# Loading the second layer's V, Z and O weights as pairs of 256 columns: a two-layer decoder step on one core

## The reference

```python
for l in range(DEPTH):                       # DEPTH = 2
    h = rmsnorm(x, g_pre[l]) * (1 + scale) + shift      # shift, scale, gate = silu(c) @ w_ada + b_ada
    y = branch(h)                            # l = 0: attention, l = 1: mLSTM
    x = x + gate * rmsnorm(y, g_post[l])

def mlstm_branch(h, w_in, b_if, g_head, w_out, S0, n0, m0):
    proj = h @ w_in                          # (2048, 8208): q 1024, k 1024, v 2048, o 2048, z 2048, gates 16
    ...                                      # 8 heads: dk = 128, dv = 256; memory S <- a S + k v^T, read by q
    hn = rmsnorm_per_head(hs) * g_head * sigmoid(o)
    out = hn * silu(z)
    return out @ w_out, S, n, m
```

## Time and profile before

| | |
|---|---|
| median of 3 runs | 2271.52 us (2266.96 to 2273.0) |
| profiled execution | 2274.41 us |
| its span, first to last instruction | 2272.8 us |
| TensorE matmuls busy | 2170.9 us (96% of the span) |
| VectorE busy | 940.9 us (41%) |
| ScalarE busy | 677.5 us (30%) |
| DMA from the SP queue | 247.87 MB, 39.6% of 16 engines' span |
| mean granted TensorE clock | 0.979 of full speed |

### The profile page before, as it was taken

How to read it: one execution, slowest core, us unless ns; L and a number is a source line. 1 busy time by engine, 2 the same in 40 slices (tenths; PEclk the granted TensorE clock), 3 DMA queues, 4 the chain that set the end, 5 groups by cost and what they waited for, 6 DMA issues and landing times.

```text
span 2272.8 us, 37219 instructions
## 1 busy us (share of the span) xinstructions
PE 2170.9 (96%) x15828; PEld 1857.0 (82%) x15828; DVE 940.9 (41%) x1430; ACT 677.5 (30%) x1135; POOL 74.9 (3%) x125
## 2 busy tenths in 40 slices
PE   5899999999999999998899999999799999999998
PEld 2689999988999555567889999999799999985576
DVE  4434645456474422234443434443243434353223
ACT  4213534435252311126221222222222222231121
POOL 1000000000000100000000000000000000001000
PEclk8999999999999999998999999999899999999999
DMA  8972222232221788854425243534343344428622
GB/s 316 384 249 80 59 75 75 65 87 57 78 57 56 261 269 286 287 173 142 73 69 117 68 118 74 112 66 94 73 104 81 100 86 94 96 83 301 220 76 98
DMA packets 290435, 298.86 MB, mean 131 GB/s; under 512 B 8705, under 2 KB 213753, under 8 KB 288649
## 3 DMA queue, kind: packets, MB, share of 16 engines
q1 hardware_dynamic: 279504, 247.87, 39.6%
q0 software_dynamic: 10496, 48.45, 6.0%
q10 hardware_dynamic: 290, 0.32, 0.1%
HBM read 277.58 MB, written 23.11 MB: 132 GB/s over the span
## 4 chain that ended last, share of the span: by engine, by line
PE 84%; DMA 9%; DVE 3%; ACT 2%; issue 1%; ACTq 0%; DVEq 0%; SPq 0%
PE PJ L852 48%; PE PJ L1135 16%; DMA raw<-in_w_in_mlstm 6%; PE MX L1063 3%; DMA obuf<-in_w_ada 2%; PE PJ L876 2%; PE MX L992 1%; PE MX L1001 1%; PE MX L1101 1%; PE MX L1015 1%; ACT w_hi L1386 1%; PE MX L1269 1%; DVE w_lo L1842 1%; PE MX L955 1%; PE MX L1326 1%
## 5 line engine op out<-in xcount | busy, mean ns | idle before, releaser
L852 PE MATMUL PJ<-h_hi,w_hi 128*128 128x272 f32 x3200 | 684.8, 295 | 8.6 <-issue 6.9
L852 PE MATMUL PJ<-h_hi,w_lo 128*128 128x272 f32 x3200 | 667.5, 290 | 0.3 <-issue 0.3
L852 PE MATMUL PJ<-h_lo,w_hi 128*128 128x272 f32 x3200 | 665.6, 290 | 0.0
L852 PEld LDWEIGHTS PJ<-h_hi,w_hi 128*128 128x128 f32 x3200 | 507.0, 190 | 25.6 <-issue 20.8
L852 PEld LDWEIGHTS PJ<-h_lo,w_hi 128*128 128x128 f32 x3200 | 508.6, 191 | 7.0 <-issue 7.0
L852 PEld LDWEIGHTS PJ<-h_hi,w_lo 128*128 128x128 f32 x3200 | 505.6, 191 | 0.6 <-issue 0.6
L1842 DVE TENSOR_TENSOR w_lo<-raw,w_hi 128x2048 fp32r<-128x2048 f32 x106 | 242.9, 2292 | 389.0 <-ACT w_hi L1386 388.8
L1386 ACT ACTIVATE w_hi<-raw 128x2048 fp32r<-128x2048 f32 x106 | 202.3, 1909 | 86.9 <-DMA raw<-in_w_in_mlstm 64.2
L1135 PE MATMUL PJ<-w_hi,h_hi 128*128 128x512 f32 x512 | 216.1, 422 | 3.5 <-DVE w_lo L2117 2.3
L1135 PE MATMUL PJ<-w_hi,h_lo 128*128 128x512 f32 x512 | 202.9, 396 | 0.0
L1135 PE MATMUL PJ<-w_lo,h_hi 128*128 128x512 f32 x512 | 202.2, 395 | 0.0
(11 more groups left out here) (380 smaller groups left out, 2038.5 us busy)
## 6 DMA issues: line engine op xcount, KB each, us to landing
arena<-in_w_ada SPq DMA_DIRECT2D x64, 1024.0 KB, 5.2
raw<-in_w_in_mlstm SPq DMA_DIRECT2D x64, 1024.0 KB, 15.7
raw<-in_w_in_attn SPq DMA_DIRECT2D x40, 1024.0 KB, 5.8
obuf<-in_w_ada SPq DMA_DIRECT2D x32, 1024.0 KB, 11.4
raw<-in_w_out_attn SPq DMA_DIRECT2D x16, 1024.0 KB, 7.5
raw<-in_w_out_mlstm SPq DMA_DIRECT2D x16, 1024.0 KB, 5.2
arena<-in_state_C POOLq DMA_DIRECT2D x8, 1024.0 KB, 15.9
out<-arena POOLq DMA_DIRECT2D x8, 1024.0 KB, 5.9
```

The source lines that it names most:

```text
L852: last = mm(PJ[:, 2 * pair + f, 0:HT], w, h[:, k, HT * f:HT * f + HT], start=(k == 0 and n == 0), stop=(k == KT - 1 and n == 2))
```

## The change

The order of a head's units becomes Q K V V Z Z O O. The two raw buffers become the two halves of one tile, `raw_all`. Q and K are loaded as before. For V, Z and O, `load_pair` brings both units' 256 columns at once: half 0 holds k tiles 0 to 7, half 1 holds k tiles 8 to 15, each a DMA of 1 MB in pieces of 256 columns, 1 KB. `w_source` picks the 128 columns of one unit out of all sixteen k tiles, for `round_hi` and `split_lo`. The waits follow from the shared tile: a pair waits until the unit just before it has been split; ACT waits for both halves; the next head's Q, and the first block of the output projection, wait until the last O has been split; and the second O's Tanh waits until VectorE has used the first one's.

```diff
-L1K = "QKVVZOZO"
+L1K = "QKVVZZOO"
...
-        raw = [sb(f"raw{i}", [P, D]) for i in range(2)]
+        raw_all = sb("raw", [P, 2 * D])
+        raw = [raw_all[:, D * i:D * i + D] for i in range(2)]
...
+        def w_source(ph, e):
+
+            if ph == "l1" and 2 <= e < len(L1K):
+                return raw_all.rearrange("p (k n) -> p k n", k=KT)[:, :, P * (e % 2):P * (e % 2) + P]
+            return raw[slot_of(ph, e)].rearrange("p (k n) -> p k n", k=KT)
...
-                split = fixed(sp, unit_no(ph, it, e, j - 1))
+                split = fixed(sp, unit_no(ph, it, e, j - 1 + (ph == "l1" and e == 0 and it[0] is not None)))
...
-                    sp.wait_ge(lo_done, UNIT0[ph] + u - 1)
+                    sp.wait_ge(lo_done, UNIT0[ph] + u - (0 if l and u == 0 else 1))
...
+            def load_pair(it, e, col):
+
+                split = fixed(sp, unit_no("l1", it, e))
+                sp.wait_ge(xt_done, 5)
+                sp.wait_ge(lo_done, split)
+                for half in range(2):
+                    sp.dma_start(raw[half].rearrange("p (k n) -> p k n", k=KT // 2),
+                                 win1[:, KT // 2 * half:KT // 2 * (half + 1), ds(col, DV)]).then_inc(w_in[half], 16)
+
...
-                    load("l1", it, e, 0, win1[:, :, ds(h * width + (start[kind] + P * seen[kind]), P)])
+                    if kind in "QK":
+                        load("l1", it, e, 0, win1[:, :, ds(h * width + start[kind], P)])
+                    elif seen[kind] == 0:
+                        load_pair(it, e, h * width + start[kind])
...
+                if ph == "l1" and 2 <= e < len(L1K):
+                    other = e + 1 - 2 * (e % 2)
+                    act.wait_ge(w_in[slot_of(ph, other)], landed_at(ph, it, other))
...
-                fn(w_hi[s][:, :], raw[s][:, :], ACT.Copy).then_inc(hi_done, 1)
+                fn(w_hi[s][:, :].rearrange("p (k n) -> p k n", k=KT), w_source(ph, e), ACT.Copy).then_inc(hi_done, 1)
...
                 if kind == "O":
+                    if seen:
+                        act.wait_ge(*freed_at("l1", it, e - 1))
...
-                    tt(w_lo[s][:, :], raw[s][:, :], w_hi[s][:, :].bitcast(F32), ALU.subtract)\
-                        .then_inc(lo_done, 1)
+                    tt(w_lo[s][:, :].rearrange("p (k n) -> p k n", k=KT), w_source(ph, e),
+                       w_hi[s][:, :].bitcast(F32).rearrange("p (k n) -> p k n", k=KT), ALU.subtract).then_inc(lo_done, 1)
```

## The result

The changed kernel takes 2380.18 us in the median of 4 runs (2375.65 to 2385.31); the kernel before, on the same chip, 2272.26 us in 4 (2266.96 to 2274.9). The ratio is 1.0479, with a 95% interval of 1.045 to 1.0507. The direction and the range were forecast; the change was forecast as +33 us and measured as +108 us. The profiled execution took 2385.31 us, its span 2383.7.

A forecast was written before the change was run, and what follows sets the result against it. Six heads were taken as bound by matmuls, two (0 and 4) by loads. Waits of 48 us, 72 with the clock, less the present 39.2 gave +33 us: 2304 us, range 2232 to 2400 us.

The forecast's parts named there:

- The ceiling, 39.2 us: Heads 0 and 4, over head 2's 115.49 us: the most that better loading can give back, 39.2 us.
- the rival in which the pairs escape: Wide pieces escape the slow pitch: pairs land within 14.6 us in every head, no waits, 2232 us; chance 0.15.
- The price of a pair: V, Z, O loads: a pair takes what its head's first V load takes now (head 0: head 4's value); chance 0.40.
- The two factors behind it (1.28 and 0.8): Pair loads: 1 KB pieces cost 1.28 times as much, closely following loads 0.8; the product is about 1.
- V and Z, 14.7 + 21.2 = 35.9 us of waits: Pair times above the room of 15.9 us in V and 14.6 us in Z, summed over the heads.
- State traffic, 12 us "in all": V window, where GpSimd stores and reloads 1 MB of state: 12 us more waiting in all, between 0 and 60.
- O: none: O pairs: no waits, as each has 22.1 us of room before O's first unit starts on TensorE.
- The clock, half as much again: TensorE after waits: the lower clock adds half as much again, making 48 us of waiting 72 us.
- "Z Z O O moves no work": Unit order Z Z O O instead of Z O Z O: moves no work, costed at nothing.
- The next head's Q, costed at nothing: Q held back until the last O is split: 24.2 us of room against a 15.7 us median load, no cost.
- the output block: Final output projection's first block, held back by one unit of over 12 us, in fast 2 KB pieces: no cost.
- Bytes alone: Rival: a pair costs two loads in a row at 0.8 each, 2449 to 2557 us; bytes or above 1.28: chance 0.20.

The follow-up runs named there:

- the kernel with short rows: Changed kernel with all second-layer unit loads taken from the first layer's input weights, rows 20,480 instead of 32,832 bytes apart: 2231.78 us.
- Without state traffic: Changed kernel with GpSimd's per-head store and reload of the samples' memory state cut from 1 MB to 4 KB each: 2337.65 us.
- the memory steps first: Changed kernel with ScalarE and VectorE doing the previous unit's memory step ahead of the next unit's rounding and splitting, from the fifth unit on: 2315.42 us.

## Why the prediction was off, step by step

- **The ceiling, 39.2 us: right.** The heads of the kernel with short rows take 930.3 us, 37.0 less than the 967.3 of before, and its 2231.78 us is the 2232 of the rival in which the pairs escape.
- **The price of a pair: right in the mean.** Without state traffic, 15.5 us against 15.7; 21.9 in head 4 against 21.5, and up to 3.9 us off in the others. The two factors behind it (1.28 and 0.8) came from far rows, so that they cancel as they did is partly luck.
- **V and Z, 14.7 + 21.2 = 35.9 us of waits: right in sum.** Without state traffic the waits ahead of units are 40.0 us: 13.8 for V and 26.3 for Z.
- **State traffic, 12 us "in all": mis-sized.** It lengthens the V pairs of heads 1 to 7 by 3.8 to 8.2 us, and costs 24.1 us of waits ahead of units (64.1 less 40.0) and, since the heads shift, about 11 more at the memory steps: 43 us of time. The text had 60 as a bound. Its 12 is what 7.5 us a head leaves over the slack of heads 3, 5 and 7 (3.7 + 3.3 + 5.0); the other heads got nothing, on the strength of heads 2 and 6, whose second V load was fast. Head 3's 7.5 us for all of heads 1 to 7 would have made 42; ahead of V alone it was 34.9 (48.7 less 13.8). With this and O's waits the odd heads, which were to stay near 115.5 us, took 122 to 144.
- **"O: none": the step that failed.** I measured O's window up to the unit's first matmul, 22.1 us (22.2 by the earlier trace rows). What needs the landing first is the memory step behind the rounding, on ScalarE's and VectorE's programs, and its window was 12.4 us in six heads and 16.4 and 16.7 in heads 0 and 4. The text named the queue ("behind ScalarE's wait for both halves stand the memory steps") and dismissed it because TensorE needs them "only in Z and O"; but the O pair is awaited just there. Measured: 28.3 us of waits where the sum had none. With 12.4 us for the window, the forecast's own prices would have given 33 (an estimate: what the first V loads of the earlier trace rows take above 12.4 us, head 0 at head 4's value).
- **The clock, half as much again: right for the whole.** The heads lie 145.9 us above the 930.3 with 97.1 us idle, a factor of 1.50; before, 37.0 us with 25.9, 1.43. By cause it differs: 65 us for 32 of waits at the memory steps, 43 for 35 with the state's traffic.
- **"Z Z O O moves no work" at no cost: wrong in the other direction.** It gives 23 us, by the columns that are in flight together.
- **The next head's Q, costed at nothing: the same slip, small.** Its 24.2 us of room ran to Q's first matmul. No unit Q waits for its load, but memory step 6 stands behind Q's rounding and waited 3.7 us, once, in head 3. With the 28.3 us of O these are the 32.0 us that putting the memory steps first removed, for 65 us of time.
- **Costed at nothing, and right:** the output block (from the heads' end to the end of the span 247.2 us, before 248.7), the strided reads (1910 and 2291 ns, before 1909 and 2292).
- **The rivals.** Bytes alone: no, half the pieces at equal bytes take about 0.7 of the time. The Trainium skill, "DMA: Bandwidth & Descriptors", section Why small descriptors are slow, gives by an estimate 35 cycles against 2 x 19 for that, 0.92; the measurement decides. Wide pieces escape: they do from the short rows and not from these. The Trainium skill, same page, section Latency and other measured facts, reports copies slowed at row pitches of 2 MiB and more, and full speed again at 4 KiB over 4 MiB. The prediction set this against the rival, but the k tiles here lie 8 KiB over 4 MiB, so the rule spoke neither way, and no run here shows its case.

With the waits of 40 + 24 + 32 + 1 = 97 us in place of 48, the forecast's own arithmetic gives 97 x 1.5 - 39 = 106 us; measured, 108. That 2380 us lies inside the stated range is luck: the range reached so far up for dearer pairs (the factor 1.28 without the 0.8), and nothing in it stood for the memory steps.

## What to carry to other kernels

When an edit makes a load start later, its window ends not at the matmul that uses the data but where some engine first needs what is queued behind the wait; list what stands behind the wait on ScalarE and VectorE and who waits for that. When two buffers become one, price the lost overlap apart from the wider pieces: here the later start, with both loads at once, took 268 us and the wider pieces gave 137 back. A transfer that ran beside the old loads must be priced beside the new, concentrated ones, at the nearest row's value, in every pass.

## What the runs showed of the hardware

The time of a 1 MB load from the 32,832-byte rows depends on which loads are in flight beside it: the same four loads of head 4 take 20.7 to 23.4 us in one order of columns and 18.3 to 32.0 in the other, 23 us of the kernel's time without any other change. Half the pieces for the same bytes took 0.73 of the time in the mean of 24 pairs. And removing 32 us of short waits gave back 65 us, as the clock then held its upper level, 2.4 GHz, for longer: the changed kernel's heads have a mean granted clock of 0.93, with the memory steps first 0.96, with short rows 0.99.
